# A hybrid layer of gated DeltaNet and attention: branch A's projection goes into the attention loop, the gate's modulation behind the scan

## The chip, the cores and the metric

The kernel runs on one core of a Trainium2 chip, as one program. The metric is the device time in microseconds (us) from its start to its end. A core has TensorE (PE, matrix products into the eight banks of PSUM), VectorE (DVE), ScalarE (ACT) and GpSimd (POOL); the sync engine (SP), ACT and POOL also issue DMA transfers. Each engine has its own queue of instructions and works through it in order; semaphores tie the queues together.

## What is computed

One layer over 512 latent tokens of 2048 channels, with 256 context tokens. With `silu(c) @ w_mod + b_mod` split into shift, scale and gate:

```python
h = rms_norm(x, norm_w) * (1 + scale) + shift          # hc the same from ctx
aq, ak, av, az, ab, aa, bq, bk, bv, bz, br = split_in(h @ w_in)
a_lat = gated DeltaNet over context, then latent tokens, both directions,
        head-wise RMS norm, times silu(az)              # 8 heads of 128
b_lat = softmax attention, 8 query heads on 2 key heads, 512 queries
        on 768 keys, times silu(bz)
g_a, g_b = split(sigmoid(br), 2)
x_new = x + gate * ((g_a * (a_lat @ w_proj_a) + g_b * (b_lat @ w_proj_b)) @ w_out)
```

All is f32. The two projections are 1024 by 2048 each, `w_out` 2048 by 2048. The modulation is a product of two rows (for the latents and for the context; of the gate only the first is used) with 2048 by 6144 weights.

## The kernel before

**Pieces.** All products with weights are cut into pieces of 512 KB of weights, in one order (`projection_plan`, L60): 64 pieces of modulation (shift and scale), 48 for the convolved q, k, v, the small `ab`, 8 for B's keys and values, 96 of gates, 16 of B's queries (`bq`), 32 of the gate's modulation (`modg`), 32 of `merge` (for each of eight groups of 256 channels two of branch A and two of branch B) and 32 of the output product. SP loads them in this order: the first 64 into four buffers, the rest into two (`raw_of`, L362).

**Three products for one.** For all but the modulation, ACT writes a rounded copy of each piece (`hi_part`, L554), DVE the remainder (`lo_part`, L862), and PE makes three fast products, high with high, high with low, low with high (`three`, L1338). The modulation is multiplied whole in f32, with two columns of `silu(c)` as the stationary operand; one f32 matmul shows as two passes in the trace. The two result rows are copied by ACT (`mod_rows`, or `modg_rows` L661), transposed by PE (`mod_cols`, L1310), and their bias is added by DVE (`modg_columns`, L1119).

**The order.** Each engine's queue is one loop over the piece number n, written out by hand, with the other work hung to fixed values of n. The steps of the scan (`gdn`) stand between matmuls of the gate pieces, four to a piece. The scan ends at `N_FIN` (piece 186); then come branch A's norm, its product with `silu(az)` and its split into `a_hi` and `a_lo` (pieces 193 to 196), beside the last gate pieces and, from piece 217, `bq`. The gates go through `gate_scratch` in HBM: ACT writes them there, POOL fetches them when wanted (`z_load`, `gates_load`). SP's weight loads run ahead of PE by two pieces.

**The attention loop** has 32 passes i, four (blocks of 128 queries) for each head h. PE's order in a pass (L1590 to L1610): the scores of i + 1; in a head's first pass `values(h - 1)`; nought to two `modg` pieces (`MODG_STEPS`, L160); in four passes transposes of further queries; then the six transposes of the probabilities of pass i. ACT's order: the exponential of i + 1 (`att_exp`), the copy of pass i's transposes, in pass 1 the squares of half of the queries, in a head's second pass `b_hi` of the head before. DVE's order: the division by the row sum of pass i (`p_norm`), the maximum of i + 1 (`att_max`), then rotation of queries in passes 4, 6, 7 and 8, and in a head's second pass `b_parts` (product with `silu(bz)`, wait for `b_hi`, remainder). Scores use banks 0 to 3, transposes 4 and 5, values 6, the modulation 7.

**After the loop** come the values of the last head, then `merge`. After its second piece, 16 small matmuls spread the gate over all rows (`gate_rows`); POOL makes their operands (L532), four buffers of them. For each two channels groups of `merge`, DVE multiplies both sums by their gates, adds them (L1272 to L1276), and the result is split into `m_hi` and `m_lo`. `x_again`, x once more for the residual sum, is loaded by POOL when the output product begins.

Of the kernel before, what the change touches and what calls it, by code (L numbers as in the profile page):

```python
# [7 lines left out]
P = 128  # L8
# [6 lines left out]
KV = 2  # L15
# [18 lines left out]
NCONST = STAGE + len(MASKED) * 2 * 16  # L34


def shape_constants():
# [8 lines left out]
    for s in MASKED:  # L46
        for backward in (0, 1):
            cols = np.arange(32)[(np.arange(32) // s) % 2 == (0 if backward else 1)]
            want = cols // s + (1 if backward else -1)
            parts.append(r // s == want[None, :])  # L50
    consts = np.concatenate(parts, axis=1).astype(np.float32)
# [8 lines left out]
def projection_plan():  # L60
# [4 lines left out]
    def group(kind, col, width, per_piece, **more):  # L65
        g = dict(kind=kind, col=col, width=width, first=len(pieces), **more)
        for k0 in range(0, KT, per_piece):
# [17 lines left out]
    for j in range(4):  # L85
        group("modg", 2 * DM + 512 * j, 512, 2, j=j)
    for j in range(8):
        for branch in (0, 1):
            g = dict(kind="merge", first=len(pieces), j=j, branch=branch)
            for k0 in (0, 4):  # L90
                pieces.append(dict(g=len(groups), kind="merge", k0=k0, nk=4, col=256 * j, width=256, branch=branch, j=j))
            g["last"] = len(pieces) - 1
            groups.append(g)
# [32 lines left out]
def build(nc, x, c, ctx, c_ctx, w_mod, b_mod, norm_w, w_in, conv_w, a_log, dt_bias, a_norm_w, q_norm_w,  # L126
# [12 lines left out]
    MODGS = [gi for gi, g in enumerate(GROUPS) if g["kind"] == "modg"]  # L139
# [6 lines left out]
    N_MODG0 = GROUPS[MODGS[0]]["first"]  # L146
    N_MERGE0 = GROUPS[MODGS[-1]]["last"] + 1
# [7 lines left out]
    whole = [p["kind"] in ("mod", "modg") for p in PIECES]  # L155
# [4 lines left out]
    MODG_STEPS = (0, 2, 1, 1, 0, 2, 2, 0)  # L160
    MODG_END = len(MODG_STEPS) - 1
    assert sum(MODG_STEPS) == 8

    def modg_pieces(i):

        n = N_MODG0 + 8 * (i // 8) + sum(MODG_STEPS[:i % 8])
        return range(n, n + MODG_STEPS[i % 8])

# [74 lines left out]
    mrow = at("mod_rows", [2, 512], A_T + 9728)  # L243
# [32 lines left out]
    mrow_g = at("mod_gate_rows", [2, 512], A_T + 8192)  # L276
# [23 lines left out]
    xr = at("x_again", [P, LT, DM], A_G + 8192)  # L300
# [5 lines left out]
    with ExitStack() as stack:  # L306
# [44 lines left out]
        def src_of(p):  # L351
            w = {"merge": (w_proj_a, w_proj_b)[p.get("branch", 0)], "out": w_out, "mod": w_mod, "modg": w_mod}.get(p["kind"], w_in)
# [15 lines left out]
        def accs_free_needed(eng, gi):  # L368
# [4 lines left out]
            if g["kind"] == "modg" and gi > MODGS[0]:  # L373
                eng.wait_ge(S("modg_cols"), MODGS.index(gi))
# [12 lines left out]
            if g["kind"] == "bq":  # L387
# [3 lines left out]
                else:  # L391
                    eng.wait_ge(S("a_tmp"), HEADS)
            if g["kind"] == "merge" and g["branch"] == 0:
                if g["j"] == 1:
# [1247 lines left out]
```

## Time and profile before

| | us |
|---|---|
| time, median of 3 runs (lowest, highest) | 2127.43 (2125.99, 2130.21) |
| the profiled execution: its time | 2123.39 |
| its span in the trace | 2121.6 |
| PE matmul busy in the span | 2048.3 (97%) |
| DVE, ACT, POOL busy | 896.3, 623.6, 196.1 |
| DMA, mean over the span | 103 GB/s |

Busy times are of one profiled execution, which took 2123.39 us, so what is worked out from the trace is to be set against that, and only then against the median. A stretch is given by its start and end in us from the start of the span. PEclk, or the granted clock, is TensorE's clock as a share of 2.4 GHz, so 0.50 is 1.2 GHz. A matmul's recorded duration holds its pipeline; the distance from one start to the next is what a stream of them costs.

### The profile page before, as it was taken

How to read it: one execution, taken by the hardware profiler on the slowest of the kernel's cores; microseconds unless marked ns; L12 is line 12 of the kernel's file. 1: busy time of each engine (PE TensorE's matmuls, PEld its weight loads, DVE VectorE, ACT ScalarE, POOL GpSimd, SP SyncE). 2: the span in 40 equal slices, each digit the busy share in tenths (PEclk: the TensorE clock that was granted, in tenths of full speed). 3: DMA queues.
4: the chain of work that ended last, by engine and by line, in shares of the span. 5: the costliest groups of instructions: out<-in, count | busy, mean ns of one | idle time of the engine just before them, and what ended most of it. 6: DMA issues, size and time to landing. Idle time of an engine off the chain costs nothing.

```text
span 2121.6 us, 39241 instructions
## 1 busy us (share of the span) xinstructions
PE 2048.3 (97%) x17376; PEld 1546.8 (73%) x17376; DVE 896.3 (42%) x1762; ACT 623.6 (29%) x1062; POOL 196.1 (9%) x328
## 2 busy tenths in 40 slices
PE   7999999999999999999999999999989889999997
PEld 2238888888777777788777878788853337888886
DVE  1324344455235445554445554622345333544333
ACT  3313221223132323233332225422353331222111
POOL 0000000000012222222121221000000011100000
PEclk9999999999999999999999999999999999999999
DMA  8862122233122222222222225443323343445332
GB/s 288 281 235 66 54 60 60 60 90 84 51 90 62 72 62 62 61 71 61 62 75 60 69 61 147 139 129 109 100 60 114 109 135 98 149 140 178 118 112 88
DMA packets 151970, 218.78 MB, mean 103 GB/s; under 512 B 9632, under 2 KB 99993, under 8 KB 150521
## 3 DMA queue, kind: packets, MB, share of 16 engines
q1 hardware_dynamic: 136777, 172.87, 27.4%
q0 software_dynamic: 7248, 29.25, 4.0%
q10 hardware_dynamic: 7776, 14.16, 1.8%
q8 instruction: 136, 2.23, 0.4%
q14 instruction: 33, 0.27, 0.0%
HBM read 197.90 MB, written 18.35 MB: 102 GB/s over the span
## 4 chain that ended last, share of the span: by engine, by line
PE 88%; ACT 5%; DVE 3%; DMA 2%; issue 1%; POOL 0%; SPq 0%; ACTq 0%; POOLq 0%; DVEq 0%
PE psum L1341 23%; PE psum L1342 21%; PE psum L1343 21%; PE psum L1439 6%; PE psum L1586 2%; PE psum L1408 2%; PE psum L1404 1%; ACT inv L628 1%; PE psum L1416 1%; PE psum L1371 1%; ACT square_out L655 1%; DMA w_raw<-w_mod_dram 1%; PE psum L1334 1%; PE psum L1422 1%; DVE w_lo L867 1%
## 5 line engine op out<-in xcount | busy, mean ns | idle before, releaser
L867 DVE TENSOR_TENSOR w_lo<-w_raw,w_hi 128x1024 fp32r<-128x1024 f32 (+1 forms) x233 | 291.2, 1250 | 670.1 <-ACT w_hi L562 669.6
L562 ACT ACTIVATE w_hi<-w_raw 128x1024 fp32r<-128x1024 f32 (+1 forms) x233 | 246.0, 1057 | 1049.2 <-PE psum L1343 1025.3
L1341 PE MATMUL psum<-h_hi,w_hi 128*128 128x512 f32 (+1 forms) x1168 | 485.8, 416 | 7.0 <-DVE w_lo L867 4.8
L1342 PE MATMUL psum<-h_lo,w_hi 128*128 128x512 f32 (+1 forms) x1168 | 459.5, 393 | 0.0
L1343 PE MATMUL psum<-h_hi,w_lo 128*128 128x512 f32 (+1 forms) x1168 | 458.8, 393 | 0.0
L1343 PEld LDWEIGHTS psum<-h_hi,w_lo 128*128 128x128 f32 (+1 forms) x1168 | 218.7, 187 | 50.7
L1341 PEld LDWEIGHTS psum<-h_hi,w_hi 128*128 128x128 f32 (+1 forms) x1168 | 219.4, 188 | 49.3 <-DVE w_lo L867 6.2
L1342 PEld LDWEIGHTS psum<-h_lo,w_hi 128*128 128x128 f32 (+1 forms) x1168 | 219.8, 188 | 34.4
L1439 PE MATMUL psum<-w_raw_mod,silu_c 128*2 128x512 f32 x256 | 113.8, 598 | 1.7 <-ACT silu_c L682 0.8
L935 DVE SCALAR_TENSOR_TENSOR conv_acc<-conv_in,convw,conv_acc 128x772 f32<-128x772 f32 x96 | 98.2, 1023 | 3.4
L1341 PE MATMUL psum<-w_hi,m_hi 128*128 128x512 f32 x256 | 99.6, 389 | 0.0
L1342 PE MATMUL psum<-w_lo,m_hi 128*128 128x512 f32 x256 | 99.6, 389 | 0.0
L1343 PE MATMUL psum<-w_hi,m_lo 128*128 128x512 f32 x256 | 99.6, 389 | 0.0
L1439 PEld LDWEIGHTS psum<-w_raw_mod,silu_c 128*2 128x2 f32 x256 | 20.4, 85 | 85.7 <-issue 71.5
L458 POOL TENSOR_TENSOR decay_rhs_hi<-consts,g_hi 128x512 fp32r<-128x512 f32 x24 | 29.0, 1209 | 533.3 <-PE psum L1343 439.0
L1341 PE MATMUL psum<-w_hi,h_hi 128*128 128x512 f32 x192 | 75.4, 393 | 2.5 <-ACT gate_stage L790 1.3
L1343 PE MATMUL psum<-hc_hi,w_lo 128*128 128x256 f32 (+1 forms) x272 | 76.8, 282 | 0.0
L1342 PE MATMUL psum<-hc_lo,w_hi 128*128 128x256 f32 (+1 forms) x272 | 76.8, 282 | 0.0
L1341 PE MATMUL psum<-hc_hi,w_hi 128*128 128x256 f32 (+1 forms) x272 | 76.3, 280 | 0.0
L1342 PE MATMUL psum<-w_lo,h_hi 128*128 128x512 f32 x192 | 74.8, 389 | 0.0
L1343 PE MATMUL psum<-w_hi,h_lo 128*128 128x512 f32 x192 | 74.7, 389 | 0.0
L484 POOL COPY invT<-inv32T 32x128 f32<-32x128 f32 x96 | 34.1, 355 | 319.2 <-DVE inv L951 314.3
(297 smaller groups left out, 2922.6 us busy)
## 6 DMA issues: line engine op xcount, KB each, us to landing
w_raw<-w_in_dram SPq DMA_DIRECT2D x168, 512.0 KB, 3.8
w_raw_mod<-w_mod_dram SPq DMA_DIRECT2D x64, 512.0 KB, 5.0
w_raw<-w_mod_dram SPq DMA_DIRECT2D x32, 512.0 KB, 3.8
w_raw<-w_out_dram SPq DMA_DIRECT2D x32, 512.0 KB, 3.7
gate_scratch<-gate_stage ACTq DMA_DIRECT2D x48, 256.0 KB, 2.5
gates<-gate_scratch POOLq DMA_DIRECT2D x32, 256.0 KB, 3.4
w_raw<-w_proj_a_dram SPq DMA_DIRECT2D x16, 512.0 KB, 3.6
w_raw<-w_proj_b_dram SPq DMA_DIRECT2D x16, 512.0 KB, 3.5
```

What stands on the lines that cost most here:

```text
L458: ins = pool.tensor_tensor(part_t[d][:], mask, g_t[:, col:col + 4].bitcast(f32).unsqueeze(2).to_broadcast([P, 4, P]), ALU.mult)
L484: pool.tensor_copy(YY[d][32 * q:32 * q + 32, :, 32 * q:32 * q + 32], YC[d][32 * q:32 * q + 32]).then_inc(S(f"diag{d}"), 1)
L562: act.activation(part(whi[i % 2], p), part(place, p), ACT.Copy).then_inc(S("w_hi"), 1)
L628: ins = act.activation(XX[d][:, u, :], YY[d][:, u, :], ACT.Copy, scale=betar[:, col:col + 1])
L867: dve.tensor_tensor(part(wlo[i % 2], p), part(raw_of(n)[0], p), part(whi[i % 2], p).bitcast(f32), ALU.subtract).then_inc(S("w_lo"), 1)
L935: ins = dve.scalar_tensor_tensor(out=a[:], in0=r[:, tap:tap + 772], scalar=w, in1=a[:], op0=ALU.mult, op1=ALU.add)
L1341: pe.matmul(out_ap, lh, rh, start=first, stop=False, skip_group_check=shared)
L1342: pe.matmul(out_ap, lh, rl, start=False, stop=False, skip_group_check=shared)
L1343: return pe.matmul(out_ap, ll, rh, start=False, stop=last, skip_group_check=shared)
L1408: ins = pe.matmul(bank4(b, 16)[own, u, :], XC[d][own, u, :], PM[d][own, u, 0:16], start=True, stop=True)
L1439: ins = pe.matmul(bank(b0)[0:2], sc2[:, p["k0"] + kk, :], part3(place, p)[:, kk, :], start=first and kk == 0, stop=last and kk == p["nk"] - 1)
L1586: ins = pe.matmul(bank(6), kvr[:, t, 256 + kv * P:256 + (kv + 1) * P], PTt[:, t, :], start=(t == 0), stop=(t == NT - 1))
```

## The change

Branch A's projection is cut anew, into 16 pieces of 128 channels by all 1024 rows, and each is done in two halves in two passes of the attention loop, in bank 7. DVE multiplies the sum by branch A's gate, and POOL writes the product back over that gate in HBM. `merge` keeps branch B alone and adds the fetched product. The `modg` pieces leave the sequence of pieces: POOL loads them into three buffers of their own, and PE does them behind the gate pieces 197 to 216. All modulation, the first 64 pieces too, puts row block k into column group k % 4, so that four partial sums of two rows each stand in one bank (zeroed beforehand); all 128 rows are copied, and a matmul with a constant selection matrix adds the four and transposes them in one. `x_again` is loaded ahead of the fifth and later gates.

```diff
+    for m in range(16):
+        group("pa", 128 * m, 128, 8, m=m, kt=8)
     for j in range(8):
+        group("merge", 256 * j, 256, 4, j=j, kt=8)
...
+    N_MODG0 = N_FIN + 11
+    MODG_AFTER = [N_MODG0 + q * (N_BQ0 - N_MODG0) // 32 for q in range(32)]
...            # accs_free_needed
+            if g["kind"] == "pa":
+                if g["m"] == 0:
+                    eng.wait_ge(S("a_lo"), HEADS)
+                    eng.wait_ge(S("kt_evac"), KV)
+                else:
+                    eng.wait_ge(S("pa_mul"), g["m"])
+            if g["kind"] == "merge":
+                if g["j"] < 2:
+                    eng.wait_ge(S("exp_done"), 31 + g["j"])
+                elif g["j"] < 4:
                     eng.wait_ge(S("grow_evac"), 4)
+                else:
+                    eng.wait_ge(S("m_psum"), 2 * (g["j"] - 3))
...            # POOL
+            def modg_load(q):
+                if q >= 3:
+                    pool.wait_ge(S("modg_used"), q - 2)
+                pool.dma_start(part3(raw_modg[q % 3], MODG[q]), src_of(MODG[q])).then_inc(S(f"modg_in{q % 3}"), 16)
+            def pa_store(m):
+                pool.wait_ge(S("pa_mul"), m + 1)
+                pool.dma_start(gate_scr[16 + m], pa_out[m % 2][:]).then_inc(S(f"pa_spill{m % 2}"), 16)
...            # ACT, attention loop
             for i in range(32):
-                if i % 8 == MODG_END:
-                    modg_rows(i // 8)
                 if i < 31:
                     att_exp(i + 1)
+                if i % 2 == 0:
+                    hi_part(N_PA0 + i // 2 + 1)
...            # DVE, attention loop
+            def pa_gated(m):
+                dve.wait_ge(S("w_used"), N_PA0 + m + 1)
+                dve.wait_ge(S(f"pa_gate{m % 2}"), 16 * (m // 2 + 1))
+                if m >= 2:
+                    dve.wait_ge(S(f"pa_spill{m % 2}"), 16 * (m // 2))
+                dve.tensor_tensor(pa_out[m % 2][:], bank(7), pa_gate[m % 2][:], ALU.mult).then_inc(S("pa_mul"), 1)
...
                 if i < 31:
                     att_max(i + 1)
-                if i % 8 == MODG_END:
-                    modg_columns(i // 8)
+                if i % 2 == 0:
+                    lo_part(N_PA0 + i // 2 + 1)
+                    if i:
+                        pa_gated(i // 2 - 1)
...            # PE, modulation
                     for kk in range(p["nk"]):
-                        ins = pe.matmul(bank(b0)[0:2], sc2[:, p["k0"] + kk, :], part3(place, p)[:, kk, :],
-                                        start=first and kk == 0, stop=last and kk == p["nk"] - 1)
+                        k = p["k0"] + kk
+                        c0 = 32 * (k % 4)
+                        ins = pe.matmul(bank(b0)[c0:c0 + 2], sc2[:, k, :], part3(place, p)[:, kk, :],
+                                        start=k < 4, stop=k >= KT - 4)
...            # PE, a "pa" piece
+                    if 0 in halves:
+                        accs_free_needed(pe, gi)
+                        pe.wait_ge(S("w_lo"), parts_made[n])
...
+                    for half in halves:
+                        for kk in range(4 * half, 4 * half + 4):
+                            ins = three(bank(7), (wh[:, kk, :], wl[:, kk, :]), (a_hi[:, kk, :], a_lo[:, kk, :]), kk == 0, kk == 7)
...            # PE, attention loop, after scores(i + 1) and values(h - 1)
-                for n in modg_pieces(i):
-                    piece(n)
-                if i % 8 == MODG_END:
-                    mod_cols(mrow_g, 7, "modg", i // 8 + 1)
+                piece(N_PA0 + i // 2, (i % 2,))
...
+            piece(N_MERGE0)
             values(HEADS - 1)
```

## Rows read from the trace of the kernel before

**Rows 1.** The page, part 4: the chain that ended last, by engine.
```profile
PE 88%; ACT 5%; DVE 3%; DMA 2%; issue 1%; POOL 0%; SPq 0%; ACTq 0%; POOLq 0%; DVEq 0%
```
**Rows 2.** Stretches: length, busy us (instructions) by engine, granted clock, DMA share, GB/s.
```profile
80.00:146.00 66.00, 64.89 (x162) 12.64 (x160) 17.40 (x44) 9.87 (x21) 0.00 (x0) 1.00 0.84 288
...
30.00:46.00 16.00, 14.72 (x61) 5.65 (x60) 2.42 (x5) 6.44 (x12) 0.81 (x2) 1.00 0.93 332
...
1554.00:1750.00 196.00, 175.59 (x605) 75.20 (x603) 83.39 (x178) 81.84 (x159) 10.11 (x18) 0.99 0.34 108
```
**Rows 3.** Order of time, PE, merge: start, duration, engine, line, instruction.
```profile
1750.83 0.40 PE L1341 MATMUL psum<-a_hi,w_hi 128*128 128x512 f32 x1
...
1760.38 0.39 PE L1341 MATMUL psum<-a_hi,w_hi 128*128 128x512 f32 x1
```
**Rows 4.** Order of time, attention loop, passes 16 and 17; and its first transposes.
```profile
1562.64 0.87 PE L1609 MATMUL psum<-consts,probs 128*128 128x128 f32 x6 [1.54 <-DVE probs L1240]
...
1652.70 5.42 PE L1586 MATMUL psum<-probsT,kv_rows 128*128 128x512 f32 x12 [0.53 <-ACT probsT L825]
...
1657.96 0.82 PE L1609 MATMUL psum<-consts,probs 128*128 128x128 f32 x6
...
1658.61 1.02 PE L1573 MATMUL psum<-att_kT,att_qT 128*128 128x512 f32 x2
...
1660.00 3.59 PE L1439 MATMUL psum<-w_raw,silu_c 128*2 128x512 f32 x8
1660.11 0.96 DVE L1224 TENSOR_REDUCE neg_max<-psum 128x1 f32<-128x768 f32 x1 [4.37 <-PE psum L1574]
...
1661.10 0.15 DVE L1225 TENSOR_SCALAR neg_max<-neg_max 128x1 f32<-128x1 f32 x1
...
1661.29 0.90 ACT L811 ACTIVATE probs<-psum,neg_max 128x768 f32<-128x768 f32 x1 [1.60 <-DVE neg_max L1225]
...
1662.09 0.19 ACT L811 ACTIVATION_READ_ACCUMULATOR probs<-psum,neg_max 128x1 f32 x1
...
1663.53 0.88 PE L1609 MATMUL psum<-consts,probs 128*128 128x128 f32 x6
...
1664.44 0.81 ACT L825 ACTIVATE probsT<-psum 128x768 f32<-128x768 f32 x1 [2.16 <-PE psum L1609]
```
**Rows 5.** Order of time, PE, small tiles of the scan (x: passes).
```profile
1191.62 0.75 PE L1401 MATMUL psum<-consts,L 32*32 32x32 f32 x64
...
1211.92 0.60 PE L1386 MATMUL psum<-inv32T,L 32*32 32x32 f32 x32
1212.45 0.50 PE L1341 MATMUL psum<-h_hi,w_hi 128*128 128x512 f32 x1
```
**Rows 6.** DMA issues: what, queue, count, KB each, median us to landing.
```profile
z_stage<-gate_scratch POOLq DMA_DIRECT2D x16, 256.0 KB, 4.1
```
**Rows 7.** Order of time, from w_hi of one piece to its w_lo.
```profile
1343.94 1.06 ACT L562 ACTIVATE w_hi<-w_raw 128x1024 fp32r<-128x1024 f32 x1 [1.65 <-PE psum L1343]
...
1345.04 1.23 DVE L867 TENSOR_TENSOR w_lo<-w_raw,w_hi 128x1024 fp32r<-128x1024 f32 x1 [2.02 <-ACT w_hi L562]
```
**Rows 8.** The chain of waits in order of time, attention loop: start, us, what.
```profile
1570.74 0.41 ACT square_out L655 x2
...
1665.14 0.63 ACT b_hi L836
1665.80 0.69 DVE b_lo L1234
...
1667.22 0.88 DVE neg_max L1224
```
**Rows 9.** Stretches of 2 us round the loop's long wait; and the values beside it.
```profile
1576.00:1578.00 2.00, 0.15 (x1) 0.00 (x0) 0.34 (x2) 1.94 (x7) 0.00 (x0) 1.00 0.36 49
...
1584.00:1586.00 2.00, 2.00 (x3) 0.69 (x3) 1.86 (x6) 0.99 (x2) 0.00 (x0) 0.50 0.00 0
...
1583.09 7.11 PE L1586 MATMUL psum<-probsT,kv_rows 128*128 128x512 f32 x12 [2.21 <-ACT probsT L825]
```

More of the change, by code:

```diff
@@ L33 @@
 MASKED = BLOCKS[1:-2]
[L34 removed]
+SEL = STAGE + len(MASKED) * 2 * 16
+NCONST = SEL + 8
 def shape_constants():
@@ L145, in build @@
     N_BQ0 = GROUPS[BQS[0]]["first"]
-    N_MODG0 = GROUPS[MODGS[0]]["first"]
-    N_MERGE0 = GROUPS[MODGS[-1]]["last"] + 1
+    N_PA0 = GROUPS[PAS[0]]["first"]
+    N_MERGE0 = GROUPS[PAS[-1]]["last"] + 1
     N_OUT0 = GROUPS[OUTS[0]]["first"]
@@ L683, in _ @@
                            ACT.Silu).then_inc(S("silu_c"), 1)
-            for n in range(N_MODG0):
+            for n in range(N_PA0):
                 hi_part(n + 1)
@@ L726, in _ @@
                         act.activation(a_hi[:, h, :], atmp[h % 2][:], ACT.Copy).then_inc(S("a_hi"), 1)
+                for k in range(4):
+                    if n == MODG_AFTER[8 * k + 7] + 1:
+                        modg_rows(k)
                 if n == GROUPS[BQS[0]]["last"] + 1:
@@ L868, in lo_part @@
                                   ALU.subtract).then_inc(S("w_lo"), 1)
+            for b in (4, 5):
+                dve.memset(bank(b), 0.0).then_inc(S("rows_zero"), 1)
             dve.wait_ge(S("const_in"), 16)
@@ L1158, in _ @@
                         a_lo_part(h)
+                if r == 11:
+                    for b in (4, 5):
+                        dve.memset(bank(b), 0.0).then_inc(S("rows_zero"), 1)
+                for k in range(4):
+                    if n == MODG_AFTER[8 * k + 7] + 2:
+                        modg_columns(k)
                 if 13 <= r < 15:
@@ L1313, in mod_cols @@
                 for q in range(4):
-                    ins = pe.transpose(bank(b, 2, 2 * q), rows_t[:, q * P:(q + 1) * P], ident[0:2, 0:2])
+                    ins = pe.matmul(bank(b, 2, 2 * q), rows_t[:, q * P:(q + 1) * P], consts[:, SEL:SEL + 2], start=True, stop=True)
                 ins.then_inc(S(f"{name}_cols_mm"), 1)
@@ L1423, in gdn, with modg_piece, piece @@
                     ins.then_inc(S(f"gp{d}"), 1)
-            def piece(n):
+            def modg_piece(q):
+                p = MODG[q]
+                if q < 16 and q % 8 == 0:
+                    pe.wait_ge(S("rows_zero"), 3 + q // 8)
+                if q >= 16 and q % 8 == 0:
+                    pe.wait_ge(S("modg_rows"), q // 8 - 1)
+                pe.wait_ge(S(f"modg_in{q % 3}"), 16 * (q // 3 + 1))
+                for kk in range(2):
+                    k = p["k0"] + kk
+                    c0 = 32 * (k % 4)
+                    ins = pe.matmul(bank(4 + q // 8 % 2)[c0:c0 + 2], sc2[:, k, :], part3(raw_modg[q % 3], p)[:, kk, :],
+                                    start=k < 4, stop=k >= KT - 4)
+                ins.then_inc(S("modg_used"), 1)
+            def piece(n, halves=(0, 1)):
                 p = PIECES[n]
@@ L1458, in piece @@
                         if kind == "merge":
-                            src = ((a_hi, a_lo), (b_hi, b_lo))[p["branch"]]
-                            b0 = 4 * (p["j"] % 2) + 2 * p["branch"]
+                            src = (b_hi, b_lo)
+                            b0 = 2 * (g["j"] % 4)
+                            if g["j"] == 0:
+                                pe.wait_ge(S("b_lo"), k + 1)
                         for j in (0, 1):
@@ L1501, in _ @@
             pe.wait_ge(S("silu_c"), 1)
-            for n in range(N_MODG0):
+            for n in range(N_PA0):
                 piece(n)
@@ L1511, in _ @@
                         mod_cols(mrow, 6 + gi % 2, "mod", gi + 1)
+                for q in range(32):
+                    if n == MODG_AFTER[q]:
+                        modg_piece(q)
+                for k in range(4):
+                    if n == MODG_AFTER[8 * k + 7] + 1:
+                        if k >= 2:
+                            pe.wait_ge(S("modg_cols"), k - 1)
+                        mod_cols(mrow_g, 6 + k % 2, "modg", k + 1)
                 r = n - N_FIN
```

140 lines of the change are left out of this document (71 added, 69 removed).

## The prediction

> **What bounds the kernel now.** I read the page first. The chain that ended last lies on PE for 88% of the span [rows 1], so TensorE (PE) sets the time nearly everywhere, and a change counts by the PE time that it adds, removes or leaves idle. Next, the table of busy time by stretch [rows 2]. From 80 to 146 us, the second half of the modulation, PE is busy without a break while the DMA engines stand at 0.84 and 288 GB/s; from 30 to 46 us, with the loads of x beside it, they reached 0.93 and 332 GB/s. The attention stretch, 1554 to 1750 us, has PE busy 175.6 of 196 us: some 20 us idle. Third, the order of time. Merge matmuls start every (1760.38 - 1750.83) / 42 = 0.2274 us [rows 3], so a piece of 24 takes 5.46 us. Inside the attention loop [rows 4] one score tile takes 1.39 us (1658.61 to 1660.00), six transposes 0.65 us (1657.96 to 1658.61), a head's values 5.26 us, and eight passes of the modulation's f32 matmuls 3.53 us, 0.44 us a pass, two passes a matmul.
>
> **The change part by part.**
>
> *Merge.* Branch A's 16 pieces leave it: -16 x 5.46 = -87.3 us. The last values and the 16 gate-row matmuls stay. VectorE's work per two channels falls while the interval halves to 10.9 us (about 4 us of its own and two splits of 1.2 us), so it stays hidden. The gates' loads double their rate and x_again (4 MB) now goes on the same POOL queue ahead of gates 4 and 5. They are needed some 20 us after it; a late one would hold VectorE's next split and then PE. I take 0, with 0 to +8.
>
> *Modulation of the gate.* The 64 matmuls leave the loop and go behind the scan between the gates' pieces, where PE has no idle time to give. Undivided they cost 32 x 4 x 0.44 = 56.5 us. In two column groups the first matmul's second pass may run beside the next matmul's first. The trace has no matmul of 128 rows in column groups. The nearest rows are the scan's small tiles [rows 5]: 32 passes in two groups took 0.53 us from their start to the next matmul, where 32 x 0.027 (a quarter of a 128-column transpose of 0.108 us) = 0.86 would be in a row, a factor of 1.63; 64 passes in four groups spanned 0.75 us against 1.73. Bounds are 28 us (both groups wholly side by side) and 60 us (no overlap, and 0.1 us at each change of tile shape). I take 56.5 / 1.63 = +35 us, by the row with two groups, since a piece has only two. Three POOL-queue buffers feed them; a 256 KB load on that queue lands in 4.1 us [rows 6], and a buffer is asked for again after about 13 us, so the loads are hidden, and so are the row copies and sums, which wait one piece each.
>
> The Trainium skill (TensorEngine Tiling, Tiling Modes) says that a change of tiling mode drains the engine, which speaks against scattering these matmuls over 20 places. The small tiles' rows above contain one such change in each direction, so their factor has it in it. The skill (TensorE: Matmul & The Clock Gate, Part 3) gives 2.38 for three column tiles of 512 columns; an estimate from it is 1.59 for two, and the sum would be the same within 1 us. No row of before shows either for these shapes.
>
> *First modulation.* The same division makes PE need less than the 1.76 us a piece that it needs now, and DMA takes over. If it ran at 332 GB/s throughout, 132 us would become about 112: -20 us. But the loads with x are already near that, and the chain of x tiles stays. Below, +3 us if PE's waits only change their name. I take -6 us.
>
> *The attention loop.* Each pass of 32 now holds half a piece of branch A's projection, 12 x 0.2274 + 0.1 = 2.83 us, in place of the 56.5 us of modulation. PE's work from the first transposes on: 32 x 0.65 transposes, 30 x 1.39 scores, 31 x 2.83 halves, 8 x 5.26 values, 4 x 0.5 query transposes = 194.3 us. The first transposes come 1.2 us later than 1562.64 [rows 4], because half a piece goes in front. With no waits values(7) would end near 1758, 8 us later than before's 1750.
>
> But a wait is added, and it is what decides. All 16 pieces accumulate in bank 7 alone, and a piece's first half waits for `pa_mul` of the piece before. VectorE does that product in an even pass only after `att_max(i + 1)` and `lo_part`; `lo_part` waits for ScalarE's `hi_part`, and that stands behind `att_exp(i + 1)`. These start from scores(i + 1), which PE issued just ahead of the waiting matmul. So PE stands through the whole chain, with its transposes, whose input has long been ready, queued behind it. Its length from the end of the scores: 0.11 to VectorE, 1.18 for both parts of the maximum to the start of the exponential, 0.99 for that with its sum (1661.29 to 1662.28) [rows 4], 0.05, 1.10 from the start of w_hi to that of w_lo, 1.23 w_lo [rows 7], 0.03, 0.69 for the product (as m_tmp and b_lo, 128x512), 0.1 to PE: 5.48 us. In passes 4, 8, ..., 28 the values (5.26 us) lie between and hide all but 0.2. In passes 6, 10, ..., 30 nothing lies between, and VectorE comes late too: it has first waited for b_hi behind the last transposes. In before the maximum starts 3.69 us after those transposes (1663.53 to 1667.22) [rows 4, 8]; then the same 5.37 us follow, and PE has 2.04 us of work: 7.0 us of waiting. In pass 2 the 16 squares of queries stand in ScalarE's queue: 1.72 from the transposes' start to the end of their copy, 16 x 0.41, 0.99, 3.20 for the links from w_hi on, less 2.04: 10.4 us [rows 4, 8]. Together 10.4 + 7 x 7.0 + 7 x 0.2 = 61 us. The chain cannot be shorter unless instructions change order (bound below 50); q_tile's seven operations on VectorE in passes 4 and 6 to 8, table loads and queueing can lengthen it (bound above 75).
>
> *The clock.* From 1576 to 1578 us PE was busy 0.15 us; after that stretch of little work the granted clock was 0.50 from 1584 to 1586 us (1.2 GHz), and the values beside it took 7.11 us where 5.26 is usual [rows 9]: 1.85 us lost. A bare wait of 7 to 11 us comes eight times, so 8 x 1.85 = 15 us; from 0 (it holds) to 25 (it stays low through the transposes and scores too).
>
> *The loads and stores added to the loop* (weights in runs of half the length, the gate in, the product out) have two pieces, over 25 us, from issue to use against some 4 us to land [rows 6]; I count 0.
>
> **Sum.** Loop: 8.1 + 61 + 15 = +84. Merge -87.3, gate's modulation +35, first modulation -6: +26 us. The profiled execution took 2123.4 us (span 2121.6), so 2149 by its own time. The three timed runs have a median of 2127.4, 4.0 higher; on it, 2153 us.
>
> **Rivals.** *The bank is not waited for* (0.14). If the product is in fact in time, because something in the queues stands otherwise than I read, the 61 and 15 us go: -50 us, 2077. For it speaks that 20 us of idle PE were there to be filled and that removing 56.5 us at a factor of 1.63 is real; it decides once the wait per pair of passes is under (61 + 15 - 26) / 15, some 3.3 us on average with its clock loss. Against it: the order of the three queues in even passes, and that the same links (b_hi, b_lo, probs, neg_max) already end waits in before [rows 8]. *The waits come but cheap* (0.13): the clock holds, DMA runs near 332 GB/s and the groups lie fully side by side: 8 + 53 - 87 + 28 - 16 = -14, 2113. *Column groups don't run side by side* (0.13), so that the change doesn't do what it says: +57 for the gate's part and 0 for the first: 8 + 61 + 15 - 87 + 57 = +54, 2181. Small tiles in other rows are no proof for tiles that share all 128 rows.
>
> **How the numbers follow.** The forecast has the other 0.60, its own range 2130 to 2175 (chain 50 to 75, clock 0 to 25, groups 28 to 45, not all at one end). The range for 8 in 10 is 2104 to 2190: it takes in the cheap case and most of that without overlap, and leaves out the case without the wait. A difference within 0.2% (4 us) can't be told from none here. Faster: 0.14, 0.09 of the cheap case, 0.03 of the forecast's low end = 0.26; same 0.08; slower 0.66.
>
> **What would show it.** In the profile after: waits of the branch-A matmuls on the product with the gate, 5 to 11 us long, in passes 2, 6, ..., 30 and almost none in 4, 8, ...; a stretch from bq to the last values of about 278 us instead of 196; granted clock 0.5 after those waits; the gate stage 35 us longer; the modulation matmuls starting less than 0.44 us apart; DMA above 300 GB/s in the first 140 us. I would be wrong if the projection's halves start right behind the scores.

## The result, and the profile after

| | before | changed |
|---|---|---|
| time, median of 4 runs each on one chip (lowest, highest), us | 2126.71 (2122.94, 2130.21) | 2140.26 (2138.26, 2142.76) |
| the profiled execution's time, us | 2123.39 | 2142.76 |
| its span, us | 2121.6 | 2141.0 |
| mean granted clock in the span | 0.995 | 0.973 |

The ratio is 1.0066, with a 95% interval from 1.005 to 1.0083: slower by 13.6 us at the median, 19.4 us between the two profiled executions.

Stretches of the changed kernel come first (length, busy time with count for PE, PE's loads, DVE, ACT and POOL, granted clock, DMA share, GB/s); they answer to [rows 2, 9].

```profile
14.00:80.00 66.00, 46.11 (x242) 17.65 (x244) 17.17 (x38) 31.41 (x54) 3.19 (x6) 0.89 0.87 297
80.00:146.00 66.00, 47.35 (x195) 12.72 (x192) 17.37 (x40) 11.82 (x23) 0.00 (x0) 0.88 0.85 288
80.00:132.00 52.00, 37.77 (x156) 6.83 (x152) 14.92 (x38) 9.22 (x20) 0.00 (x0) 0.88 0.90 310
1319.80:1572.50 252.70, 249.26 (x1153) 187.41 (x1152) 86.04 (x130) 75.68 (x132) 24.90 (x37) 1.00 0.54 168
1573.00:1860.00 287.00, 223.78 (x867) 154.66 (x866) 110.66 (x206) 94.65 (x170) 27.30 (x50) 0.88 0.23 72
1631.00:1633.00 2.00, 0.04 (x1) 0.04 (x1) 1.93 (x3) 0.04 (x1) 0.00 (x0) 0.50 0.00 0
```

The attention stretch has become 287 us long where it had 196 (5.5 us of the 287 are a `merge` piece that now stands ahead of the last values), with PE idle for 63 us of it and a mean clock of 0.88. In the second half of the first modulation PE is busy 47 of 66 us instead of 65. The DMA figures of that row, 0.85 and 288 GB/s, are those of before, but the stretch reaches beyond the modulation, whose last matmul now starts at 136.1 us. From 80 to 132 us, where both kernels are in it, the share is 0.90 against 0.85 and the rate 310 against 291 GB/s. The fourth row is the gate stage, from the scan's last outputs to the end of `bq`. The third and the fourth row have these counterparts in before:

```profile
80.00:132.00 52.00, 51.90 (x130) 10.21 (x128) 17.23 (x43) 9.18 (x20) 0.00 (x0) 1.00 0.85 291
1324.70:1553.80 229.10, 223.72 (x993) 184.35 (x992) 83.38 (x123) 72.58 (x127) 4.31 (x8) 0.99 0.40 117
```

What PE's matmuls waited for in the changed kernel's loop (total us, times, longest), and, second fence, in its first 146 us:

```profile
PE psum L1379 <- DVE pa_stage L1274: 56.3, 9, 10.5
PE psum L1650 <- ACT att_qT L826: 5.9, 4, 1.5
PE psum L1650 <- ACT att_kT L832: 1.0, 2, 0.9
```

```profile
PE psum L1506 <- DMA w_raw_mod<-w_mod_dram: 29.3, 35, 4.5
```

Now pass 6 in the changed kernel's chain of waits, from the transposes of pass 5 to the branch-A matmul that waited (start, us, what):

```profile
1624.54 0.67 PE psum L1683 x6
...
1625.94 0.63 ACT b_hi L864
1626.59 0.69 DVE b_lo L1267
...
1627.39 0.62 DVE probs L1280
1628.02 0.88 DVE neg_max L1257
...
1629.13 0.78 issue
1629.90 0.19 ACT probs L839
1630.10 0.95 ACT w_hi L588
...
1631.14 1.08 issue
1632.22 0.70 DVE pa_stage L1274
...
1632.96 0.79 PE psum L1379
```

```profile
1631.08 1.23 DVE L892 TENSOR_TENSOR w_lo<-w_raw,w_hi 128x1024 fp32r<-128x1024 f32 x1 [2.00 <-ACT w_hi L588]
```

The chain is read upwards from the matmul at 1632.96. It waited for the product with the gate (`pa_stage`), which stands on VectorE behind `w_lo`; the "issue" of 1.08 is `w_lo` itself, 1.23 us from 1631.08, whose releaser is `w_hi` on ScalarE; that stands behind the exponential; that needs the maximum; and VectorE was late for the maximum because it had waited for `b_hi`. Waits of this kind, in PE's order of time (idle time before in brackets), those of passes 6 and 14 with the start of the work behind the half piece:

```profile
1599.77 0.79 PE L1379 MATMUL psum<-a_hi,w_hi 128*128 128x512 f32 x1 [10.55 <-DVE pa_stage L1274]
...
1632.96 0.79 PE L1379 MATMUL psum<-a_hi,w_hi 128*128 128x512 f32 x1 [6.47 <-DVE pa_stage L1274]
...
1638.24 1.12 PE L1683 MATMUL psum<-consts,probs 128*128 128x128 f32 x6
1639.20 1.02 PE L1650 MATMUL psum<-att_kT,att_qT 128*128 128x512 f32 x2
...
1650.99 0.50 PE L1379 MATMUL psum<-a_hi,w_hi 128*128 128x512 f32 x1 [0.47 <-DVE pa_stage L1274]
...
1700.76 0.79 PE L1379 MATMUL psum<-a_hi,w_hi 128*128 128x512 f32 x1 [6.46 <-DVE pa_stage L1274]
...
1704.99 0.60 PE L1622 MATMUL psum<-consts,bq_rows 128*128 128x128 f32 x4
```

In pass 6 the half piece takes 1638.24 - 1632.96 = 5.28 us where the one at 1650.99, which waited only 0.5 us, takes 2.86, and its transposes 1639.20 - 1638.24 = 0.96 us instead of 0.65. In pass 14, after as long a wait, the half piece takes only 1704.99 - 1700.76 = 4.23 us. The granted clock was 0.50 (1.2 GHz) in the wait of pass 6 (the last of the changed kernel's stretches above) and still from 1633 to 1635 us. In pass 14 it came back within the half piece:

```profile
1701.00:1703.00 2.00, 2.00 (x5) 1.57 (x6) 0.43 (x1) 0.00 (x0) 1.08 (x2) 0.50 0.71 203
1703.00:1705.00 2.00, 2.00 (x9) 1.54 (x8) 0.00 (x0) 0.00 (x0) 0.00 (x0) 0.82 0.94 319
```

Last, two of the 20 places in the gate stage where the gate's modulation now stands, PE's order of time (x: passes):

```profile
1378.59 0.39 PE L1381 MATMUL psum<-h_hi,w_lo 128*128 128x512 f32 x1
1378.91 1.03 PE L1473 MATMUL psum<-w_raw_modg,silu_c 128*2 128x512 f32 x4
1379.87 0.50 PE L1379 MATMUL psum<-h_hi,w_hi 128*128 128x512 f32 x1
...
1392.74 0.39 PE L1381 MATMUL psum<-h_hi,w_lo 128*128 128x512 f32 x1
1393.06 1.04 PE L1473 MATMUL psum<-w_raw_modg,silu_c 128*2 128x512 f32 x8
1394.03 0.50 PE L1379 MATMUL psum<-h_hi,w_hi 128*128 128x512 f32 x1
```

Twice the passes take the same time. Without them the next matmul would start 0.23 us after the last; it starts 1.28 and 1.29 us after it, so a place costs 1.05 us whether it holds one piece (8 places) or two (12 places).

Where the 19.4 us come from, by marks in the two traces (us from the span's start; a step is the change in the time since the mark before):

| | before | changed | step |
|---|---|---|---|
| first of the scan's projection matmuls | 147.7 | 139.5 | -8.2 |
| the scan's last outputs | 1324.7 | 1319.8 | +3.3 |
| last copy of `bq` done, queries' transposes begin | 1553.8 | 1572.5 | +23.6 |
| last values (one merge piece of 5.5 us taken out) | 1749.7 | 1853.7 | +85.3 |
| end | 2121.6 | 2141.0 | -84.6 |

### The profile page after: what moved, and what is told of

Read it like the earlier page. It is cut to its first block, busy times and chain, and to the rows that moved or that the text cites. A ratio compares the mean times of both kernels' runs of the same rounds, so it can differ in the third digit from the quotient of the medians.

```text
span 2141.0 us, 39410 instructions
## 1 busy us (share of the span) xinstructions
PE 1993.5 (93%) x17424; PEld 1546.4 (72%) x17424; DVE 896.2 (42%) x1766; ACT 623.4 (29%) x1062; POOL 237.7 (11%) x392
## 4 chain that ended last, share of the span: by engine, by line
PE 84%; DMA 5%; ACT 5%; DVE 4%; issue 2%; POOL 0%; SPq 0%; ACTq 0%; POOLq 0%; DVEq 0%
PE psum L1379 23%; PE psum L1381 21%; PE psum L1380 21%; DMA w_raw_mod<-w_mod_dram 4%; PE psum L1663 2%; PE psum L1446 1%; PE psum L1442 1%; PE psum L1506 1%; ACT w_hi L588 1%; ACT inv L654 1%; PE psum L1454 1%; PE psum L1409 1%; PE psum L1683 1%; DVE w_lo L892 1%; PE psum L1473 1%
## 5 line engine op out<-in xcount | busy, mean ns | idle before, releaser
L1379 PE MATMUL psum<-a_hi,w_hi 128*128 128x512 f32 x128 | 61.9, 484 | 56.3 <-DVE pa_stage L1274 56.3
L1506 PE MATMUL psum<-w_raw_mod,silu_c 128*2 128x512 f32 x256 | 67.2, 708 | 30.1 <-DMA w_raw_mod<-w_mod_dram 29.3
L1379 PEld LDWEIGHTS psum<-a_hi,w_hi 128*128 128x128 f32 x128 | 27.8, 218 | 70.4 <-DVE pa_stage L1274 64.8
```

What stands on the lines that cost most here:

```text
L1379: pe.matmul(out_ap, lh, rh, start=first, stop=False, skip_group_check=shared)
L1506: ins = pe.matmul(bank(b0)[c0:c0 + 2], sc2[:, k, :], part3(place, p)[:, kk, :], start=k < 4, stop=k >= KT - 4)
```

## The experiments

The theory: the halves of branch A's projection wait for bank 7, because VectorE does the product with the gate behind the splits of an even pass, which hang on that pass's scores; that and the low clock behind each wait cost more than the rest gains. The rivals: the price lies in the gate stage, in the loads, or in PE's added work in the loop. Ratios are to the kernel before, on the same chip. The kernel before had medians of 2126.7, 2124.3 and 2122.9 us beside the changed kernel, the first four experiments and the next four, so a difference from the changed kernel's 2140.26 us is uncertain by up to 4 us. By the ratios the 55.7, 25.0, 9.5 and 15.3 us that follow for four of the experiments are 52, 22, 5 and 12.

**The product one pass earlier.** All else as changed.

```diff
                 if i % 2 == 0:
                     lo_part(N_PA0 + i // 2 + 1)
-                    if i:
-                        pa_gated(i // 2 - 1)
+                else:
+                    pa_gated(i // 2)
```

> One move: DVE takes the product of bank 7 with the gate at the end of the odd passes, right behind the maximum, instead of behind the splits of the even passes. Nothing is left out. Theory (PE waits for bank 7 through maximum, exponential, w_hi, w_lo and product): the nine waits of the branch-A matmuls on the product (56 us) and their low clock go, the stretch from bq to the last values falls from 281.6 to about 205 us (PE's own work there is 194 plus 10 at the start), the whole to 2060 to 2075 us. Rival (the loop is long because DVE and ACT, now with the splits and the product, set the pace of a pass): the stretch stays above 250 us and the whole above 2110; the waits only change their name to probs or neg_max.

Measured: 2084.57 us (2083.88 to 2087.89), ratio 0.982 (0.9802 to 0.9838). One instruction per piece, moved in VectorE's queue, is worth 55.7 us, and the changed kernel turns from slower to faster. The waits for the product are gone from the trace; what is left on PE in the loop and after it (total us, times, longest):

```profile
PE psum L1649 <- ACT att_qT L826: 8.1, 4, 2.0
PE psum L1682 <- DVE probs L1280: 6.3, 3, 3.3
PE psum L1696 <- POOL gate_lhs L559: 2.0, 3, 0.9
```

It came out some 10 us above what I had written for it. The transposes now wait in passes 3 and 7 (3.3 and 2.6 us) for probabilities whose division is late on VectorE: in pass 3 behind a `w_lo` that waited 7.5 us for `w_hi`, in pass 7 behind `w_lo` and the rotation of queries (1627.0 to 1631.6 us). The scores wait four times 2.0 us for the copies of later queries, 1.5 in the changed kernel.

**The splits in odd passes, the product left where it was.**

```diff
-                if i % 2 == 0:
+                if i % 2 == 1:
                     hi_part(N_PA0 + i // 2 + 1)
...
-                if i % 2 == 0:
+                if i % 2 == 1:
                     lo_part(N_PA0 + i // 2 + 1)
-                    if i:
-                        pa_gated(i // 2 - 1)
+                elif i:
+                    pa_gated(i // 2 - 1)
```

> One move: w_hi and w_lo of the next piece are made in the odd passes, the product stays in the even passes behind the maximum. Nothing is left out. Theory (the wait is a chain whose links add): without the exponential, w_hi and w_lo between (0.99 + 1.10 + 1.23 and hand-overs) the wait in passes 6, 10, ... is 3.69 + 1.18 + 0.03 + 0.69 + 0.1 - 2.04 = 3.6 us instead of 7 to 8, that of pass 2 under 2 instead of 10.5; together some 30 us less of waiting and 5 to 10 less of low clock: 2095 to 2110 us. Rival (the product is late by itself, because bank 7 is single and read by DVE, whatever stands ahead of it): within 10 us of 2140.

Measured: 2115.28 us (2110.73 to 2118.77), ratio 0.9962 (0.995 to 0.9974), worse than expected. The same row now reads:

```profile
PE psum L1379 <- DVE pa_stage L1274: 31.8, 9, 4.2
```

So the splits make 24.5 of the 56.3 us; the rest stays with the maximum, behind which the product still stands.

**One column group.** The modulation's matmuls all in column group 0, as before the change; the rest as changed.

```diff
-                        c0 = 32 * (k % 4)
+                        c0 = 0
                         ins = pe.matmul(bank(b0)[c0:c0 + 2], sc2[:, k, :], part3(place, p)[:, kk, :],
-                                        start=k < 4, stop=k >= KT - 4)
+                                        start=k == 0, stop=k == KT - 1)
```

> One change: all modulation matmuls use column group 0, in sequence, everything else as in the changed kernel (zeroed bank, 128 copied rows, selection matrix). Theory (adjacent column groups run wholly side by side: the 20 places cost about 1.1 us each, 24 us together): they cost 56.5 + 2 us again, the gate stage is 34 us longer, the first modulation goes back from about 126 to about 133 us: 2175 to 2185 us in all. Rival (the 24 us are mostly changes of tile shape and loads, the side by side running gives little): under 2155.

Measured: 2195.04 us (2190.98 to 2197.9), ratio 1.0336 (1.0314 to 1.0357), 10 to 20 us above the expectation. A double piece in its trace, and the gate stage:

```profile
1369.88 3.59 PE L1473 MATMUL psum<-w_raw_modg,silu_c 128*2 128x512 f32 x8 [1.64 <-DVE psum L1188]
1373.40 0.50 PE L1379 MATMUL psum<-h_hi,w_hi 128*128 128x512 f32 x1
```

```profile
1337.30:1627.50 290.20, 286.82 (x1154) 194.52 (x1153) 86.50 (x130) 76.07 (x132) 24.91 (x37) 1.00 0.47 146
```

Eight passes take 3.59 us again, not 1.04, and the stage costs 61.1 us over before, not 23.6. In its order of time a place with one piece costs 1.90 us and a place with two 3.62 us. Its waits in the loop are the changed kernel's (56.2, 9, 10.5), so the two parts are separate. The scan's projections begin at 155.9 us, 8.2 us later even than in before. PE hardly waits for loads there (0.3 us); its own work has grown. The selections are busy 7.4 us where the small transposes had 2.8, and the same 256 passes of the modulation are busy 117.4 us where they had 113.8, at a clock of 0.89 from 30 to 46 us and 0.93 from 80 to 100 us, 1.00 in both stretches of before.

**The kernel before with column groups, and nothing else.** The same rows, the zeroed banks and the selection matrix, put into the kernel before, whose gate's modulation stays in the loop.

```diff
-                        ins = pe.matmul(bank(b0)[0:2], sc2[:, p["k0"] + kk, :], part3(place, p)[:, kk, :],
-                                        start=first and kk == 0, stop=last and kk == p["nk"] - 1)
+                        k = p["k0"] + kk
+                        c0 = 32 * (k % 4)
+                        ins = pe.matmul(bank(b0)[c0:c0 + 2], sc2[:, k, :], part3(place, p)[:, kk, :],
+                                        start=k < 4, stop=k >= KT - 4)
```

> The kernel before with the column groups alone: modulation of the gate stays in the attention loop, branch A's projection stays in merge. Nothing is left out. Theory (first modulation is then set by DMA, and in the loop a piece of two matmuls costs 0.9 instead of 1.76 us, of which part only becomes idle time, as the loop already idles 20 us): first modulation -6 to -8, loop -10 to -25: 2095 to 2110 us. Rival (the loop is set by the chain scores, maximum, exponential, division, and PE's modulation work fills its gaps): only the first modulation gains, 2117 to 2122.

Measured: 2102.89 us (2096.47 to 2103.32), ratio 0.9896 (0.9874 to 0.9918). This part alone is a gain of 1.04%, some 22 us. The loop shrinks from 195.9 to 179.8 us, though its modulation now waits for loads:

```profile
PE psum L1447 <- DMA w_raw<-w_mod_dram: 17.4, 12, 2.5
```

**The product early, the remainder of b a pass later, both splits later.** `b_parts` keeps the product with `silu(bz)`; the wait for `b_hi` and the remainder (`b_rest`) go one pass on, `hi_part` goes behind an even pass's copies, `lo_part` into the odd pass. Its change on VectorE, in part, against the first experiment's kernel:

```diff
-                if i % 2 == 0:
-                    lo_part(N_PA0 + i // 2 + 1)
-                else:
-                    pa_gated(i // 2)
+                if i % 2 == 1:
+                    lo_part(N_PA0 + i // 2 + 1)
+                    pa_gated(i // 2)
...
+                if i % 4 == 2 and i >= 6:
+                    b_rest(i // 4 - 1)
```

> The early product of e1 and three more moves, nothing left out: DVE makes b_lo one pass later (behind the maximum), ACT makes w_hi at the end of the even passes instead of ahead of the copy of the transposes, DVE makes w_lo in the odd passes. Theory (e1's loop of 218.8 us holds some 14 us of waits and their low clock: in passes 4h + 2 the query transposes and the next scores wait behind b_hi, b_lo, the maximum, the exponential and w_hi, 3 us each): loop 204 to 209 us, 2068 to 2076 in all. Rival (those waits only move to the next link, since DVE and ACT have the same work per pass): within 4 us of e1's 2084.6.

Measured: 2066.26 us (2065.28 to 2070.67), ratio 0.9734 (0.9719 to 0.9749), at the good end of the expectation: 18 us on top of the first experiment. In its loop the waits of the transposes have shrunk from 6.3 to 0.8 us, those of the scores from 8.1 to 5.9, and one of the values for its copied transposes (3.2 us) is new:

```profile
PE psum L1686 <- DVE probs L1282: 0.8, 1, 0.8
```

**Ten operands for the gate's rows instead of four**, on the last one.

```diff
-    gcb = [at(f"gate_lhs{i}", [P, P], A_T + 8192 + 512 * i) for i in range(4)]
+    gcb = [at(f"gate_lhs{i}", [P, P], A_T + 8192 + 512 * i) for i in range(10)]
...
-                if k >= 4:
-                    pool.wait_ge(S("grow_mm"), k - 3)
+                if k >= 10:
+                    pool.wait_ge(S("grow_mm"), k - 9)
```

> e5 and ten instead of four buffers for the operands of the 16 gate-row matmuls, which POOL fills ahead. Nothing is left out. Theory (behind the first four PE waits for POOL, 0.65 us a matmul, and runs the next piece at 1.2 GHz): 9.9 us from the first to the last of them become about 4.5, and 1.5 us of low clock go: 5 to 7 us under e5. Rival (POOL fills them only after the gates' loads, so no more than four are ready): as e5.

Measured: 2065.58 us (2064.21 to 2070.21), ratio 0.9731 (0.9716 to 0.9746): nothing that can be told from the kernel with four. Yet the 16 matmuls did become shorter. With four operands, then with ten:

```profile
L1700 PE MATMUL psum<-consts,gate_lhs x32: 270/377/583, 1787.4 to 1797.3; 128*128 128x128 f32 x32
```

```profile
L1700 PE MATMUL psum<-consts,gate_lhs x32: 270/275/378, 1793.7 to 1798.9; 128*128 128x128 f32 x32
```

9.9 us became 5.2, but the stage began 6.3 us later in this profiled execution, 5.0 us of which were there from the first modulation on (137.6 against 132.6 us). That is taken up by the last experiments.

**The changed kernel with the remainder of b a pass later**, and nothing else (`b_rest` as above).

> The changed kernel with one move: DVE makes b_lo one pass later, at the end of the pass. Nothing is left out. Theory (in passes 6, 10, ... VectorE comes to the maximum 1 to 1.5 us late, because it waited for b_hi): the waits for bank 7 there fall from about 6.5 to 5.3 us, 7 to 10 us in all, the low clock behind them stays: 2130 to 2134 us. Rival (the maximum waits for the scores alone): 2140.

Measured: 2130.79 us (2128.73 to 2138.46), ratio 1.0043 (1.0028 to 1.0057), as expected, 9.5 us below the changed kernel; `b_hi`'s part of the waits is 56.3 - 46.5 = 9.8 us:

```profile
PE psum L1384 <- DVE pa_stage L1276: 46.5, 9, 10.5
```

**The changed kernel with its waits filled.** PE multiplies something of no use into a free bank while it would wait, so that only the clock differs.

```diff
+                if i % 4 == 2:
+                    pe.wait_ge(S("exp_done"), i + 1)
+                    for _ in range(24 if i == 2 else 14):
+                        pe.matmul(bank(0, 256), qhT[:, h, 0:P], khT[:, 0, 0:256], start=True, stop=True)
                 piece(N_PA0 + i // 2, (i % 2,))
```

> The changed kernel with matmuls whose result nobody reads (14, in pass 2 24, of 256 columns in f32, 0.43 us each) put into PE's queue where it waits for bank 7 in passes 2, 6, ..., 30. Nothing is left out. They fill 6 of 6.5 us (10.3 of 10.5). Theory (the granted clock of 0.50 behind the waits costs 2.5 to 3 us each time, 20 to 24 in all): the clock stays 1.00 there, the waits end as before, 2117 to 2124 us. Rival (the waits alone cost, the matmuls behind them are slow for another reason): 2140 or more.

Measured: 2124.96 us (2122.6 to 2134.08), ratio 1.0011 (0.9999 to 1.0023): 15.3 us less than changed, for the same chain of waits, and 1 us above the expected range. From the queries' transposes to the end of the last values it takes 270.0 us where the changed kernel took 286.7 in its first profiled execution and 286.3 in its second: 16.3 to 16.7 us less. Pass 6 in its order of time:

```profile
1625.53 6.21 PE L1677 MATMUL psum<-att_kT,att_qT 128*128 128x256 f32 x28
1632.16 0.50 PE L1379 MATMUL psum<-a_hi,w_hi 128*128 128x512 f32 x1 [0.42 <-DVE pa_stage L1274]
...
1635.02 0.81 PE L1687 MATMUL psum<-consts,probs 128*128 128x128 f32 x6
```

The half behind the wait takes 2.86 us, not 5.28, and the transposes' row 0.81 where it was 1.12 in the same view.

**The first ten operands ahead of the last store**, on the kernel with ten: POOL makes them in pass 31.

```diff
+                if i == 31:
+                    pool.wait_ge(S("qt_ready"), HEADS)
+                    for k in range(10):
+                        pool.tensor_scalar(gcb[k][:], ones, GATE[:, k:k + 1], None, ALU.mult).then_inc(S("gcb"), 1)
...
-            for k in range(KT):
-                if k >= 10:
-                    pool.wait_ge(S("grow_mm"), k - 9)
+            for k in range(10, KT):
+                pool.wait_ge(S("grow_mm"), k - 9)
```

> The previous combination (product early, rest of b and the halves late, ten gate operands: 2065.6 us) with the first ten of the gate's sixteen operands made on POOL in pass 31, ahead of the last store of the product and of the eight loads that stand in front of them there. Theory (the gate's operands are late because of their place in POOL's queue: in the trace of that combination they start at 1787.1, right behind eight loads that wait for the last store's landing, and take 11.5 us, while PE is through with the loop by then): with ten ready before the last pass, PE does the sixteen gate products without waiting for POOL, the stage from there to the next matmul falls from 9.9 to 4 to 5.5 us, and the product matmuls behind it start at the higher clock; 2058 to 2062 us. Rival: the projection behind them waits in any case for the first loads of the spilled gates, which land no earlier than before, so the stage only changes what it waits for; 2064 to 2067 us.

Measured: 2066.12 us (2065.36 to 2068.06), ratio 0.9725 (0.9708 to 0.9741): the same as without it. The theory fails. Its POOL rows and PE's:

```profile
L554 POOL TENSOR_SCALAR gate_lhs<-consts,gate_cols x10: 595/602/1438, 1770.6 to 1777.9; 128x128 f32<-128x128 f32 x10
L561 POOL TENSOR_SCALAR gate_lhs<-consts,gate_cols x6: 594/600/1387, 1794.2 to 1798.1; 128x128 f32<-128x128 f32 x6
L1702 PE MATMUL psum<-consts,gate_lhs x32: 270/275/377, 1793.7 to 1799.0; 128*128 128x128 f32 x32
```

The 9.9 us in my expectation was the stage with four operands; with ten made late it had been 5.2 already. Here ten were ready 16 us ahead, but the other six need buffers that PE frees only from 1793.7 on, so the 16 matmuls take 5.3 us again.

**Three kernels profiled once more**, for the first stage: the combination with four operands, with ten, and the changed kernel.

> A second profiled execution of the combination with four gate operands, for its first stage alone. In its first one the first matmul of the scan's projections by the fp32 pieces started at 132.6 us, in those of the two kernels with ten operands at 137.6 and 135.6; the three differ in nothing that runs before 1770 us. Theory (the start of that stage moves by some us from execution to execution, whatever the kernel, as its loads land): the time at which it starts differs from 132.6 by 1 us or more here. Rival (it belongs to the kernel): 132 to 133.2 us again.

> A second profiled execution of the combination with ten gate operands. Theory (the first stage's end moves from execution to execution): its first such matmul starts at another time than 137.6, by 1 us or more, and from there to the span's end it takes the same as in its first execution within 1 us, 1925.9 us, against 1931.1 for four operands: the ten operands are worth about 5 us, hidden in the totals by a late first stage. Rival (it belongs to the kernel): 137 to 138.2 us again, and the two effects cancel in every execution.

> A second profiled execution of the changed kernel, for the first stage: in the first one the scan's first projection matmul began at 139.5 us, against 147.7 before the change. Theory (column groups save about 5 to 8 us there, with some us from execution to execution): 136 to 143 us. Rival (that difference was mostly chance): 144 us or later.

Measured: 2073.63, 2068.22 and 2138.51 us, once each, while before took 2123.49. The first projection matmul starts at 141.1, 137.3 and 133.9 us, against 132.6, 137.6 and 139.5 in their first executions; 133.9 is below what either side had expected of the changed kernel. For four operands and for the changed kernel the start moved by 8.5 and 5.6 us with not an instruction changed; for ten it came back at its place, so of the rivals "it belongs to the kernel" holds nowhere as a rule, though one pair alone would have pointed to it. The expectation that the two executions with ten would agree within 1 us from there on did not come true. From there to the span's end it is 1931.1 and 1930.7 us with four operands, 1925.9 and 1929.1 with ten: worth 2 to 5 us, less than this stage's scatter. In the twelve profiled executions with column groups in the first modulation the start lies between 132.6 and 142.5 us, with a mean of 137.9; before has one, 147.7.

## Why the prediction was right

It said 2153 us, with slower at 0.66; the median is 2140.26, inside both the range and the forecast's own 2130 to 2175, and 13 us below the number itself. Some 6 of these 13 us come from the terms below, the other 6 from the two profiled executions, which lie 19.4 us apart where the medians lie 13.6 apart. By its steps:

*Merge*: -87.3 forecast, -84.6 measured from the last values to the end. Of the 2.7 us, 1.2 are the 16 gate-row matmuls, 9.9 us long instead of 8.7: in the term I took them to stay as they were.

*The wait for bank 7*: 61 forecast, 56.3 measured, in nine waits at the predicted places: 10.5 in pass 2, 6.5 in each of passes 6, 10, ..., 30 where I had 7.0, and between them a single one of 0.5. The chain is the one derived from the queues. The first two experiments, which each move one part of it, show it as the cause: 55.7 us with the product early; 25.0 us with only the splits moved.

*The clock*: 15 forecast, within 0 to 25. Against 2.86 us for a half and 0.65 for its transposes, the low clock cost 2.3 us in pass 2 (1604.91 - 1599.77 = 5.14 for the half), 2.7 in pass 6 (5.28 and 0.96), 2.7 in pass 10 and, in passes 14 to 30, 1.4, 2.8, 2.0, 1.6 and 1.4 us: 16.8 us together. Filling the waits gave the same from the queries' transposes to the last values, 16.3 to 16.7 us. The 15 was near for a reason that is partly luck. I had taken one loss of 1.85 us for all eight waits; it was larger where the clock stayed low through the half and what stands behind it, and smaller where it came back within the half.

*The rest of the loop*: 8.1 forecast. With the waits for bank 7 and the clock taken out, 85.3 - 56.3 - 16.8 = 12.2 us are left, 4 more. What the sum leaves out altogether is the wait of the scores for the copies of later queries, four times 1.5 us (5.9 us in the waits above), though the trace of before has 6.5 us of it. Where it overstates is a score tile ahead of a half, 1.11 us from start to start where it has 1.39. Waits 4.7 us shorter, 1.8 us more for the clock and these 4 us nearly cancel, and the loop came to +85.3 where +84 was forecast.

*The gate's modulation*: +35 forecast, bounds 28 to 60, +23.6 measured. This is the step that failed, and the measurement lies outside its own bounds. "A piece has only two groups" is true, but neighbouring pieces stand together at 12 of the 20 places, and there all four groups are at work: eight passes in 1.04 us. My factor of 1.63 was right for a single piece (4 x 0.44 = 1.76 us became 1.05, a factor of 1.68) and wrong for a double one (3.53 became 1.05, a factor of 3.4). The row that the 1.63 came from was also read too kindly. Its 0.53 us start with the first small tile and leave out the way in, 0.33 us from the matmul before it (1211.59 to 1211.92) where 0.23 is usual, so it holds one change of shape and not both. The sum of the places is 20 x 1.05 = 21 us. The four selections, which stood in the loop before, add about 0.9 us each, 3.5 in all, and PE's waits in the stage fell from 5.3 to 3.3 us, 1.6 of them for the zeroed banks. That is 22.5 of the 23.6 us. The lower bound supposed two groups wholly side by side and was therefore no bound. With one column group the same sum is 8 x 1.90 + 12 x 3.62 + 3.5 - 2.0 = 60.1, where 61.1 was measured. The loads were priced from rows of 256 KB; these are of 512 KB and took 5.1 us to land (median), and PE waited for none of them.

*The first modulation*: -6 forecast, -8.2 at its end in the pair of profiles, -4.9 at the end of the scan; the mean over the executions would make it -10 against a single one of before. DMA did take over, as forecast, with 29.3 us of waits, and the rate above 300 GB/s that was to show it came narrowly: 305 GB/s from 14 to 136 us, far from the 332 of the best case. From 140 to 144 us the clock is 0.60 and 0.55 (projection rows of 0.63 us instead of 0.39), which my -6 did not have in it; some six such matmuls cost about 1.3 of the 3.3 us lost by the end of the scan, and the rest was not traced. In the second execution 5.1 us were lost there.

The Trainium skill's rule that a change of tiling mode drains the engine (TensorEngine Tiling, Tiling Modes) was set against the small tiles' factor. The trace agrees that a place costs more than its streams: four passes over two groups, or eight over four, would need 0.88 us (4 x 0.44 / 2) and cost 1.05. With one column group a place costs 1.90 and 3.62 us for streams of 1.76 and 3.53, so 0.14 and 0.09 us of such a surcharge are there without any division. No run here separates a drain from the rest of the 0.17 us. The Trainium skill's 2.38 for three column tiles (TensorE: Matmul & The Clock Gate, Part 3) lies between the 1.68 for two and the 3.4 for four measured here; no run has three.

Of the rivals, "the waits come but cheap" was right that the groups lie side by side and wrong on the clock and the DMA rate; the two others did not occur. In sum: -84.6 + 23.6 + 85.3 - 4.9 = +19.4, against +26. The gate's modulation, overpriced by 11.4 us, is the one term far off; the loop, the first modulation and merge came 1.3, 1.1 and 2.7 us above their terms and take 5 of it back.

The change was then slower for one reason, a wait made by order in a queue and the clock it lost. With the product early the kernel is 1.8% faster than before; the column groups alone account for 1.04%. The best kernel measured is the one with the product early and the rest of b and the splits late: 2066 us, 2.7% below before.

## What to carry to other kernels

When an engine's in-order queue releases a buffer that another engine needs, walk back from the release through everything that stands ahead of it in that queue, and ask whether any of it depends on what the waiting engine has just issued; if so, the whole chain is exposed, however short the releasing instruction is. Price such a wait with the clock that follows it, here 1.4 to 2.8 us more for 6.5 to 10.5 us of idleness. When neighbouring pieces of narrow matmuls can stand together, count the column groups of the place, not of the piece.

## What the runs showed of the hardware

Matmuls of 128 rows by 2 columns over 512 columns in four column groups ran wholly side by side: eight f32 passes in 1.04 us, where in one group they took 3.59, and four passes in two groups took 1.03.

Behind the eight idle stretches of 6.5 to 10.5 us on PE the granted clock was 0.50, and the half piece of 12 matmuls took between 4.21 and 5.29 us instead of 2.86. With the same stretches filled with matmuls it took 2.86 (pass 6), and the clock from the queries' transposes to the last values was 1.00 in the mean instead of 0.88.

While PE waited 29 us for the modulation's loads, the DMA engines moved 305 GB/s at a share of 0.89 from 14 to 136 us, from 100 to 110 us 345 GB/s at 0.97, and a 512 KB load took 5.8 us to land (median). In a second execution of the same kernel it was 313, then 264 GB/s, the second row taking in 12 us after the stage's end at 133.9 us; from 80 to 126 us it was 318:

```profile
14.00:80.00 66.00, 47.98 (x262) 18.19 (x260) 17.26 (x39) 31.52 (x55) 3.19 (x6) 0.92 0.90 313
80.00:146.00 66.00, 46.07 (x205) 16.34 (x202) 17.27 (x40) 11.99 (x23) 0.00 (x0) 0.95 0.78 264
```

This stage, once it is bound by loads, ends at times up to 10 us apart from execution to execution of nearly the same program, as much as some of the experiments' changes are worth. What sets that is open.
